# A two-block transformer kernel on one core: the last MLP chunk before the second block in token halves, and the relative-bias rows made at that boundary

## The reference, cut to what matters

```
# first block, end
h = h + sq_relu_mlp(rms_norm(h, norm2_g), w_up, w_down)      # relu(u @ w_up)**2 @ w_down, 4096 hidden
x = rms_norm(h, final_norm_g)
# second block
h = rmsnorm(x, g_norm1) * (1 + scale1) + shift1
proj = h @ w_in                                              # q, k, v of both attentions, index q and k, gates
y_fox = forgetting_attention(q_f, k_f, v_f, cumsum(log_sigmoid(f_logit + b_forget)))
# indexer_sparse_attention, per query block:
bias = rel_bias[t5_bucket(dist)]                             # 32 buckets x 8 heads, dist = t - s
logits = q . k / sqrt(64) + bias, masked to the selected keys; softmax; @ v
```

## Time and profile before

| | us |
|---|---|
| median of 3 runs | 1351.82 (1351.14 to 1351.84) |
| the profiled execution's own time | 1352.54 |
| its span | 1350.7 |
| PE busy | 1339.7 (99% of the span) |
| POOL busy | 563.0 (42%) |
| DVE busy | 756.1 (56%) |
| ACT busy | 525.9 (39%) |

### The profile page before, as it was taken

One profiled execution on the slowest core, in us unless ns is written; L12 is line 12 of the kernel. 1 busy time (PEld: TensorE's weight loads), 2 busy tenths in 40 slices (PEclk: granted clock), 3 DMA queues, 4 the chain that ended last, 5 costly groups with the idle time before them and its releaser, 6 DMA issues.

```text
span 1350.7 us, 18066 instructions
## 1 busy us (share of the span) xinstructions
PE 1339.7 (99%) x6376; PEld 1094.2 (81%) x6380; DVE 756.1 (56%) x1085; ACT 525.9 (39%) x830; POOL 563.0 (42%) x230
## 2 busy tenths in 40 slices
PE   9999999999999999999999999999999999999998
PEld 8888878888888888886877777888878888888887
DVE  4555578475664655877788774434563241432355
ACT  6344234422323224254366665232355133142333
POOL 5334344454553635524222223444434534345351
PEclk9999999999999999999999999999999999999999
DMA  7232245555655645423212323333423423324221
GB/s 230 80 97 78 91 130 171 164 167 177 198 168 163 183 143 166 112 91 95 63 56 86 95 63 94 109 94 105 129 73 100 125 78 109 93 79 123 78 94 63
DMA packets 212807, 155.74 MB, mean 115 GB/s; under 512 B 8932, under 2 KB 193760, under 8 KB 212744
## 3 DMA queue, kind: packets, MB, share of 16 engines
q1 hardware_dynamic: 212280, 154.43, 38.4%
q10 hardware_dynamic: 464, 0.48, 0.1%
HBM read 152.75 MB, written 4.74 MB: 117 GB/s over the span
## 4 chain that ended last, share of the span: by engine, by line
PE 53%; DVE 1%; ACT 1%; issue 0%; POOL 0%; ACTq 0%; DVEq 0%
PE ps L581 28%; PE ps L1127 11%; PE ps L1071 3%; PE ps L1008 3%; PE ps L987 1%; PE ps L974 1%; PE ps L1157 1%; PE ps L960 1%; PE ps L961 1%; PE ps L947 0%; PE ps L964 0%; PE ps L921 0%; PE ps L925 0%; PE ps L922 0%; PE ps L1096 0%
## 5 line engine op out<-in xcount | busy, mean ns | idle before, releaser
L542 POOL TENSOR_TENSOR w_lo<-raw,w_hi 128x1024 fp32r<-128x1024 f32 x222 | 560.0, 2530 | 758.1 <-ACT w_hi L1213 738.0
L581 PE MATMUL ps<-u_hi,w_hi 128*128 128x512 f32 x944 | 378.5, 401 | 0.8 <-POOL w_lo L542 0.5
L581 PE MATMUL ps<-u_hi,w_lo 128*128 128x512 f32 x944 | 368.3, 390 | 0.0
L581 PE MATMUL ps<-u_lo,w_hi 128*128 128x512 f32 x944 | 367.5, 389 | 0.0
L1213 ACT ACTIVATE w_hi<-raw 128x1024 fp32r<-128x1024 f32 x222 | 231.6, 1053 | 289.3 <-PE ps L581 116.8
L581 PEld LDWEIGHTS ps<-u_hi,w_lo 128*128 128x128 f32 x944 | 177.2, 188 | 37.7
L581 PEld LDWEIGHTS ps<-u_hi,w_hi 128*128 128x128 f32 x944 | 178.1, 189 | 36.3 <-issue 1.6
L581 PEld LDWEIGHTS ps<-u_lo,w_hi 128*128 128x128 f32 x944 | 177.6, 188 | 34.9 <-issue 1.0
L581 PE MATMUL ps<-y_hi,w_hi 128*128 128x512 f32 x320 | 125.3, 391 | 0.1
L581 PE MATMUL ps<-y_hi,w_lo 128*128 128x512 f32 x320 | 124.5, 389 | 0.0
L581 PE MATMUL ps<-y_lo,w_hi 128*128 128x512 f32 x320 | 124.5, 389 | 0.0
(11 more groups left out here) (317 smaller groups left out, 1878.8 us busy)
## 6 DMA issues: line engine op xcount, KB each, us to landing
raw<-w_in SPq DMA_DIRECT2D x69, 512.0 KB, 3.7
raw<-w_mlp SPq DMA_DIRECT2D x64, 512.0 KB, 3.8
adaw<-w_ada SPq DMA_DIRECT2D x32, 768.0 KB, 4.6
raw<-w_up SPq DMA_DIRECT2D x32, 512.0 KB, 6.1
raw<-w_down SPq DMA_DIRECT2D x32, 512.0 KB, 5.5
raw<-w_out SPq DMA_DIRECT2D x16, 512.0 KB, 4.2
bias_rows<-bias_rows SPq DMA_DIRECT2D x4, 635.0 KB
xtok<-x SPq DMA_DIRECT2D x4, 512.0 KB, 7.3
```

The costliest lines, as they stand in the source:

```text
L542: pool.tensor_tensor(w_lo[:, s, :], raw[:, s, :], w_hi[:, s, :], ALU.subtract).then_inc(lo_ready[s], 1)
L581: last = pe.matmul(ps[0:cols, bank, :], w[:, s, c], r[:, k, :], start=(k == ks[0] and w is w_hi and r is r_hi), stop=(k == ks[-1] and w is ...
```

## The change

It changes two places and moves the transfers between them.

1. `bias_rows_made` leaves the first retention pair, where only the turning of `vrow` stays (`vec_turned`). The two products now stand on PE between `roots_turned(0)` and `roots_turned(1)`, with the second one's output in rows 32 to 39 of the same bank. ACT's two copies stand after its copy of `rfin`. The value rows of the second block wait for these copies before they write that bank.
2. The two products that nothing reads are gone. In the last MLP chunk DVE multiplies and adds in two halves of 256 tokens, and ACT squares in two halves. PE's four last sums wait for the front half first and for the back half before the third.
3. The loads of `oneh` and `rbias` come later on SP. `brow_copy` and `brow_spread(0)` are issued after the loads of attention pair 0, and `brow_spread(1)` to `(3)` after `tab_load` of pairs 1 to 3 (pair 1's was issued earlier). DVE's wait for `brow_out` before the first block's output projection is gone.

```
-            brow_copy()                          # after ret_loads(1)
-            brow_spread(0)                       # after the last ret_loads
-            brow_spread(1)
-            brow_spread(2)
-            brow_spread(3)
...
             att_loads(0)
             sp.wait_ge(sem("ada_sum"), 4)
-            sp.wait_ge(sem("brow_out"), 16 * (NQ + 1))
+            brow_copy()
+            brow_spread(0)
             sp.wait_ge(sem("forget_out"), 16)
             tab_load(0)
             tab_load(1)
...
             for g in range(1, 2 * NQ):
                 att_loads(g)
+                if g == NQ:
+                    sp.wait_ge(sem("brow_out"), 16 * (NQ + 1))
                 if g >= 2:
                     tab_load(g)
+                if g < NQ:
+                    brow_spread(g)
...
-                for _ in range(2):
-                    pe.matmul(ps[:, SB, 0:2 * P], ones[:], small[:, 0:2 * P], start=True, stop=True)
-                pe.wait_ge(sem("norm_sq"), sums_before("n3") + KC)
                 pe.wait_ge(sem("squares"), 4)
                 for i in range(NT):
+                    if i == 0:
+                        pe.wait_ge(sem("front_sq"), 1)
+                    if i == NT // 2:
+                        pe.wait_ge(sem("norm_sq"), sums_before("n3") + KC)
...
             def bias_rows_made():

                 pe.wait_ge(sem("bias_in"), 32)
-                pe.matmul(ps[0:HEADS, SB, :], rbias[:], oneh[:, 0:T], start=True, stop=True)
-                pe.matmul(ps[0:HEADS, OU, 0:P], rbias[:], oneh[:, T:NREL], start=True, stop=True
+                wait(pe, bank_free[2], st_idx.turn(2, 0))
+                pe.matmul(ps[0:HEADS, 2, :], rbias[:], oneh[:, 0:T], start=True, stop=True)
+                pe.matmul(ps[32:32 + HEADS, 2, 0:P], rbias[:], oneh[:, T:NREL], start=True, stop=True
                           ).then_inc(sem("brow_done"), 1)
...
-            bias_rows_made()
+            vec_turned()
             unit(st_ret, 1, 0, u_hi, u_lo)
             unit(st_ret, 2, 0, u_hi, u_lo)
-            pe.wait_ge(sem("brow_read"), 2)
...
             roots_turned(0)
+            bias_rows_made()
             roots_turned(1)
...
+                        if last and m == KC - 1:
+                            front, back = slice(0, T // 2), slice(T // 2, T)
+                            dve.tensor_tensor(nt[:, 0, front], ps[:, s, front], factor[:, front], ALU.mult
+                                              ).then_inc(sem("front_x"), 1)
+                            dve.tensor_tensor(nt[:, 0, back], ps[:, s, back], factor[:, back], ALU.mult
+                                              ).then_inc(bank_free[s], 1)
+                            dve.wait_ge(sem("front_x"), 1)
+                            dve.tensor_tensor(xres[:, m, front], nt[:, 0, front], xres[:, m, front], ALU.add
+                                              ).then_inc(sem("front_x"), 1)
+                            dve.wait_ge(bank_free[s], st.turn(s, q * 4 + 2 + i) + 1)
+                            dve.tensor_tensor(xres[:, m, back], nt[:, 0, back], xres[:, m, back], ALU.add
+                                              ).then_inc(sem("mlp_x"), 1)
+                            modulation(0)
+                            continue
```

More of the change, by code:

```diff
@@ L268, in build @@
         vrow = sb("vrow", [NVEC, P], where=pre)
-        oneh = sb("oneh", [BUCKETS, NREL], where=pre)
-        rbias = sb("rbias", [BUCKETS, HEADS], where=pre)
         pre.close()
@@ L276, in build @@
         r1 = sb("r1", [P, T], where=mix)
+        oneh, rbias = sb("oneh", [BUCKETS, NREL], where=mix), sb("rbias", [BUCKETS, HEADS], where=mix)
+        sb("to_rows", [P, 1504], where=mix)
+        fbrow = sb("fbrow", [HEADS, NREL], where=mix)
         r1sq = qf
@@ L406, in _ @@
             ret_loads(1)
-            brow_copy()
+            sp.dma_start(oneh[:], tab[0:BUCKETS, TAT["onehot"]:TAT["onehot"] + NREL]).then_inc(sem("bias_in"), 16)
+            sp.dma_start(rbias[:], rel_bias_2).then_inc(sem("bias_in"), 16)
             with sp.Fori(2, NQ) as j:
                 ret_loads(j)
-            brow_spread(0)
             with sp.Fori(0, NQ) as j:
@@ L1015, in value_slot @@
                             if s == 0 and kk == 0:
+                                if r == 0 and i == 2:
+                                    pe.wait_ge(sem("brow_read"), 2)
                                 pe.wait_ge(bank_free[i], st_idx.turn(2, 0) if r == 0 and i == 2 else st_val.turn(i, r))
@@ L1233, in square, with last_square @@
                                ).then_inc(sem("norm_sq"), 1)
+            def last_square(name, m, x0):
+                act.wait_ge(sem("front_x"), 2)
+                act.wait_ge(sem("total"), sums_before(name) + m)
+                act.activation(nsq[:, m % 2, 0:T // 2], xres[:, m, 0:T // 2], ACT.Square).then_inc(sem("front_sq"), 1)
+                act.wait_ge(sem("mlp_x"), x0 + m + 1)
+                act.activation(nsq[:, m % 2, T // 2:T], xres[:, m, T // 2:T], ACT.Square).then_inc(sem("norm_sq"), 1)
             def row_copy(n, bank, i, c):
@@ L1328, in _ @@
             act.activation(r1[:], ps[:, SA, :], ACT.Copy).then_inc(sem("r1_ready"), 1)
-            act.wait_ge(sem("brow_done"), 1)
-            act.activation(fbrow[:, 0:T], ps[0:HEADS, SB, :], ACT.Copy, scale=HD ** 0.5).then_inc(sem("brow_read"), 1)
-            act.wait_ge(sem("brow_done"), 2)
-            act.activation(fbrow[:, T:NREL], ps[0:HEADS, OU, 0:P], ACT.Copy, scale=HD ** 0.5).then_inc(sem("brow_read"), 1)
+            act.wait_ge(sem("vec_turned"), 1)
             act.activation(vec[:, KC:NVEC], ps[:, OU, P + KC:P + NVEC], ACT.Copy).then_inc(sem("vec_ready"), 1)
@@ L1456, in down @@
                                 ahead(st_idx, 0, 0)
-                            square(next_norm, m, "mlp_x", mlp_before(name) + (NF - 1) * KC)
+                            if m < KC - 1:
+                                square(next_norm, m, "mlp_x", mlp_before(name) + (NF - 1) * KC)
+                            else:
+                                last_square(next_norm, m, mlp_before(name) + (NF - 1) * KC)
                 def last_copies(s):
@@ L1501, in _ @@
             act.activation(rfin[:], ps[:, 3, :], ACT.Copy).then_inc(sem("root_f"), 1)
+            act.wait_ge(sem("brow_done"), 1)
+            act.activation(fbrow[:, 0:T], ps[0:HEADS, 2, :], ACT.Copy, scale=HD ** 0.5).then_inc(sem("brow_read"), 1)
+            act.activation(fbrow[:, T:NREL], ps[32:32 + HEADS, 2, 0:P], ACT.Copy, scale=HD ** 0.5
+                           ).then_inc(sem("brow_read"), 1)
             for s in range(2):
@@ L2078, in down @@
                             add_square(next_norm, m)
-                        if last and m == KC - 1:
-                            modulation(0)
                 up(0)
```

11 lines of the change are left out of this document (3 added, 8 removed).

## The result

| | before | changed |
|---|---|---|
| median of 5 runs (us) | 1351.61 (1351.14 to 1351.84) | 1367.28 (1366.98 to 1371.39) |
| profiled execution: own time, span | 1352.54, 1350.7 | 1367.88, 1366.1 |
| PE busy (share of the span) | 1339.7 (99%) | 1343.2 (98%) |
| PE's wait of L578 (L581 before) for POOL's `w_lo`, longest one | 0.5 | 6.7 |

The changed kernel is slower: the ratio is 1.0118, with an interval of 1.0107 to 1.0129. Over the whole program PE's share hardly moves. The list of waits and the chain of waits (part 4 of the page) of the changed kernel do name the new thing. The columns of the waits are the sum in us, how often, and the longest.

The account below looks back on a forecast made before the run. PE, busy 99% of the span, was taken as the bound. From the profiled 1352.54 us, -1.17 - 0.75 + 14.4 + 3.4 gave 1368.4; runs' median lying 0.72 lower made it 1367.7 us, range 1362.9 to 1374.4.

Parts of the forecast that it names:

- The spreads: Attention pairs 3 and 4: loads queued behind spreads land late, PE waits 7.2 us each; +14.4 us for both.
- The number of engines: Spread copies in attention: outermost dimension of 2 heads gives two DMA engines, so each copy takes 12.7 us.
- The clock behind the stalls: After each of the two attention waits PE's clock drops to 1.2 GHz; 1.7 us each, +3.4 us.
- The first retention pair: Two bias products leave PE's work there; -1.17 us, bounds 0.9 and 1.3.
- The boundary: Between the blocks, removing unread products and halving the last chunk gives -0.75 us, at worst -0.45; clock loss costed at nothing.
- bias products: Moved to the block boundary, they fit PE's wait before the first index product; 0 us, at worst +0.24.
- a rival with a chance of 0.05: Clock falls at the block boundary, where unread products kept PE busy; 1.7 us on top, 1369.4 us; chance 0.05.
- The fall in the index branch: Existing drop to 1.2 GHz after PE's 1.14 us wait, 1.7 us of PE work, assumed to stay.
- Faster: No attention stall, and the index branch's 1.2 GHz stretch goes away, another 1.7 us: 1348.2 us; chance 0.05.
- Early spreads at no cost: Spreads 0 and 1 delay no load that attention pairs 1 and 2 need in time; 0 us, at worst +4.

Follow-up runs that it names:

- e2: Changed kernel with each spread as two transfers of 128 rows, 128 outermost, instead of one of 2 x 127, at the same places; 1350.58 us.
- e5: Changed kernel with spreads 2 and 3 issued by ACT in its own queue, called one pair too late; 1363.27 us.
- e9: Kernel before plus one unused copy of a spread's shape directly ahead of attention pair 3's loads; 1360.88 us.
- e10: Changed kernel with spreads 2 and 3 issued by ACT in its own queue, at about the times SP issued them; 1356.84 us.
- e1: Changed kernel with each later spread issued right behind its pair's loads, ahead of the wait for scores and the table load; 1350.53 us.
- e11: Changed kernel with one spread of all 8 heads at the place of spread 0 and no others; 1353.57 us.
- e7: Kernel before without its two unread products, nothing else changed; 1353.23 us.
- e4: Kernel before with the last MLP chunk in two halves and no unread products; 1352.48 us.
- e6: Kernel before with the last MLP chunk in two halves, unread products kept; 1351.62 us.

## Why the prediction was right

It forecast 1367.7 us, and 1367.28 was measured. By its own steps:

- **The spreads: right.** Landings of 17.8 and 19.1 us behind a spread were carried over, and 17.7 and 18.8 were measured. PE waited 6.71 and 5.68 us against 7.2 each. In the first, each link is off by 0.1 to 0.2: the landing (17.7), the way from the cast to PE's product (703.68 to 707.22, 3.54 us against 3.66), and PE, which came 14.9 us behind the table's issue against 14.7. In the second, PE came only 17.0 us behind it (712.32 to 729.32), so that more of the lateness was hidden.
- **The number of engines: right, and it mattered.** By the Trainium skill ("DMA: Bandwidth & Descriptors", why a DMA increments its semaphore by 16) the outermost dimension sets the engines. The shares of 0.13 with 2 heads and 0.52 with 8, and the landing of 6.2 us in e2 with 128 rows outermost, agree.
- **The clock behind the stalls: mechanism right, size low.** The term was 1.7 us each, and about 2.6 and 2.4 were measured. I had priced it from the fall after a wait of 1.14 us, where PE worked some 3.4 us at 1.2 GHz; after the waits of 6.7 and 5.7 us it was 5.2 and 4.7 us. The source was also weak: the wait of 1.14 us stands in all 14 traces, and the fall behind it in one. The clock did fall behind each of the long waits of the changed kernel, e5, e9 and e10 (2.8 to 6.8 us).
- **The first retention pair: right.** -1.17 was forecast. The stretch from 37.06 to 38.64 became 37.61 to 37.87, which is 1.32 us less, just over my upper bound of 1.3.
- **The boundary: the step that failed.** The prediction said: "At the boundary before, waits of 0.42 us and less left the clock at full speed, and I cost this at nothing." With the clock held, the term is right (-0.84 against -0.75, bias products 0). In the changed kernel the clock fell and the stretch became 0.56 us longer. The prediction had this as a rival with a chance of 0.05. It came in four of the six kept traces with this boundary, and a low mean clock in 18 of 22 executions of e1 and e2. Why it comes is open.
- **What it cancelled against.** The fall in the index branch was taken as fixed. It is absent from the changed kernel's trace, so PE gained 1.58 us between the boundary and the table of pair 2. The rival "Faster" had held that possible. With the boundary's miss of 1.3 us (+0.56 in place of -0.75), it came out nearly even. The total is as close as it is partly because of this pair of errors, and because the waits were 2.0 us shorter and the clock 1.6 us dearer than their terms. All this compares one trace with one trace. That the first of these pairs came out even is luck.
- **Early spreads at no cost: right.** PE's wait at pair 1 was 0.5 us, as before. e11 shows that this holds for the narrow copy only.

## What to carry to other kernels

When a DMA is moved, ask how many engines its outermost dimension gives it and which load stands behind it; its bytes alone say little. A copy of 0.65 MB that went unnoticed beside the MLP cost 9.3 us ahead of one load with 4.2 us of slack ahead of its cast and 1.35 us behind it. Either put the large dimension outermost (the 128 rows of e2), or issue it right behind a group of loads, where the queue would be empty.

Treat "unread" matmuls as part of the timing: take them out alone, and compare enough executions with the clock of each beside it. A gain of 0.84 us that one trace shows can be less in the median if a clock fall of 1.4 to 1.6 us becomes more frequent with it.

## What the runs showed of the hardware

- A load in another engine's queue is held too, somewhat less long: landings of 13.7 and 13.9 us beside a two-engine copy, 17.0 and 18.1 behind one in the same queue, 5.0 to 5.3 with none.
- The issue itself stalls as well: the first load behind the spread held SP for 5.91 us of the 12.23 us of the pair, against 0.38 us in e1, and in e10, where the copy stands in ACT's queue.
- The granted clock is not the same in all executions of one program. e1's mean was 0.999 in 2 executions, 0.998 in 7 and 0.997 in 2. In the traces the kernel before fell at 618 and e7 at 583, while e4 and e6 did not fall ahead of their end. The Trainium skill ("TensorE: Matmul & The Clock Gate", loop structure) has an idle PE drop to half rate. At the boundary of the changed kernel it dropped while PE was busy with many matmuls of one or two columns and the long ones of `ada_rows` (busy 1.00 in each stretch from 580 to 587).
